# Banded attention moved from a stage of its own into the projection of its layer

## The reference

```
x  = x + 0.5 * norm(swiglu(norm(x)))                  # FFN 1, 2 x 2816 wide
p  = norm(x) @ w_in                                   # 768 + 1032 + 1024 columns
y_attn  = sliding_window_gqa(rope(q), rope(k), v)     # 8 query heads, 2 key heads of 64, window 128, sinks
y_mlstm = mlstm(silu(conv4(q, k)), v, gates)          # 4 heads
y_rwkv  = rwkv7(u + (shift(u) - u) * mu)              # 4 heads; u: the last 1024 columns of p
x  = x + norm(concat(y_attn, y_mlstm, y_rwkv) @ w_out)
x  = x + 0.5 * norm(swiglu(norm(x)));  then a gated embedding term
```

## Time and profile before

| | |
|---|---|
| Median of 3 runs | 3319.95 us (3317.6 to 3321.46) |
| The profiled execution, its own time | 3315.65 us |
| Its span, first to last instruction | 3313.8 us |
| PE busy | 3106.2 us, 94% |
| DVE, ACT, POOL busy | 42%, 33%, 5% |
| Mean granted TensorE clock | 0.950 of full |

### The profile page before, as it was taken

How to read it: one execution, slowest core, us unless ns; L and a number is a source line. 1 busy time by engine, 2 the same in 40 slices (tenths; PEclk the granted TensorE clock), 3 DMA queues, 4 the chain that set the end, 5 groups by cost and what they waited for, 6 DMA issues and landing times. The chain is left out here.

```text
span 3313.8 us, 42013 instructions
## 1 busy us (share of the span) xinstructions
PE 3106.2 (94%) x17718; PEld 2614.0 (79%) x17718; DVE 1385.5 (42%) x1867; ACT 1109.9 (33%) x1566; POOL 175.5 (5%) x145
## 2 busy tenths in 40 slices
PE   8999998877999999999999678899999989999999
PEld 7888886657888888888887548788887878888887
DVE  3333414556333245333332554523326247545542
ACT  3232322333322235232222332422225345434431
POOL 0000004500000000000000630000000000000000
PEclk9999999669999999999999759899999989999999
DMA  3333321001123342233413000223333210112222
GB/s 132 99 96 108 108 64 54 1 9 64 53 89 96 112 130 77 82 96 108 136 36 93 1 9 3 98 69 101 109 103 120 68 46 23 60 61 96 96 96 83
DMA packets 71483, 255.28 MB, mean 77 GB/s; under 512 B 8056, under 2 KB 9208, under 8 KB 71296
## 3 DMA queue, kind: packets, MB, share of 16 engines
q1 hardware_dynamic: 71296, 252.59, 23.8%
HBM read 250.46 MB, written 2.10 MB: 76 GB/s over the span
## 5 line engine op out<-in xcount | busy, mean ns | idle before, releaser
L206 PE MATMUL ps<-h_hi,w_space 128*128 128x512 f32 (+3 forms) x5440 | 1505.2, 363 | 17.1 <-DVE h_lo L304 17.1
L206 PEld LDWEIGHTS ps<-h_hi,w_space 128*128 128x128 f32 x5440 | 981.7, 190 | 177.8 <-DVE h_lo L304 20.3
L194 DVE TENSOR_TENSOR w_space<-w_raw,w_space 128x1024 fp32r<-128x1024 f32 x440 | 536.3, 1225 | 1222.0 <-ACT w_space L187 1221.5
L206 PE MATMUL ps<-h_lo,w_space 128*128 128x512 f32 (+3 forms) x2720 | 986.0, 363 | 0.0
L187 ACT CAST w_space<-w_raw 128x1024 fp32r<-128x1024 f32 x440 | 458.0, 1047 | 1122.1 <-PE ps L206 726.0
L216 PE MATMUL ps<-w_space 128*128 128x512 f32 x3312 | 767.9, 393 | 15.9 <-DVE w_space L194 15.0
L216 PEld LDWEIGHTS ps<-w_space 128*128 128x128 f32 x3312 | 626.5, 190 | 147.6 <-issue 11.6
L206 PEld LDWEIGHTS ps<-h_lo,w_space 128*128 128x128 f32 x2720 | 516.4, 190 | 77.9
L579 ACT CAST w_space<-act_p 128x512 fp32r<-128x512 f32 x88 | 54.6, 621 | 187.4 <-DVE act_p L591 172.4
L594 DVE TENSOR_TENSOR w_space<-act_p,w_space 128x512 fp32r<-128x512 f32 x88 | 61.0, 693 | 69.8 <-ACT w_space L579 69.8
L591 DVE TENSOR_TENSOR act_p<-act_s,ps 128x512 f32<-128x512 f32 x88 | 60.0, 681 | 71.3 <-PE ps L206 71.3
(11 more groups left out here) (324 smaller groups left out, 2732.1 us busy)
## 6 DMA issues: line engine op xcount, KB each, us to landing
w_raw<-in_w_ffn_in SPq DMA_DIRECT2D x176, 512.0 KB, 3.6
w_raw<-in_w_ffn_out SPq DMA_DIRECT2D x88, 512.0 KB, 3.6
w_raw<-in_w_in SPq DMA_DIRECT2D x64, 512.0 KB, 3.7
w_raw<-in_w_up SPq DMA_DIRECT2D x44, 512.0 KB, 3.3
w_raw<-in_w_out SPq DMA_DIRECT2D x24, 512.0 KB, 3.7
w_raw<-in_w_down SPq DMA_DIRECT2D x22, 512.0 KB, 3.3
w_raw<-in_w_ple_gate SPq DMA_DIRECT2D x16, 512.0 KB, 4.8
gain_pre<-in_gains_pre SPq DMA_DIRECT2D x10, 512.0 KB, 4.5
```

The costliest lines, as they stand in the source:

```text
L194: nc.vector.tensor_tensor(self.lo(n), self.raw[:, n % SLOTS, :], self.hi(n).bitcast(F32), ALU.subtract).then_inc(self.lo_ready, 1)
L206: m = nc.tensor.matmul(c.ps[:, bank, t], part[:, cols], moving[:, k, t], start=(k == 0 and i == 0), stop=(k == KD - 1 and i == 2))
```

## The change

The stage is gone. A class `WindowAttention` holds the same operations, with their waits, and a class `MixProj` calls them in numbered steps from the projection: `steps_after(n)` gives the steps that follow tile n. Steps 3 to 5 (constants, rope of k and the first q) follow tiles 3 to 5, one a tile. From tile 6 on there are two steps a tile: the first stands behind tile n and the second halfway through tile n+1, between its matmuls 12 and 13. Step 6+2h is `rough_scores(h)` and `values(h-1)`, step 7+2h is `scores(h)` (and `turn_back` in steps 11, 15 and 19), so the eight heads take the halves of tiles 7 to 14, and values(7) follows tile 14. Tiles 15 to 22 carry no step. The last `turn_back` follows tile 22.

The tiles stand in another order (k, q, v, mLSTM qk, rwkv, mLSTM v, o, gates). From tile 4 on they use two PSUM banks in turn, and attention has the other six; `scores` has one pair of banks, not two. The bodies of `rough_scores`, `values`, `exponents`, `maxima` and `normalise` issue the same instructions as before. The masks are loaded by SP, in the first FFN's down product, into rows of `c.y`. POOL's convolution and its token shift both follow in the projection, tile by tile as these are stored; the token shift leaves the mLSTM stage. ACT now copies a tile out before it splits the next weight unit; before it was the other way round.

```diff
     for k in range(KD):
+        if halfway is not None and k == KD // 2:
+            halfway()
...
+class MixProj(Proj):
...
+    def bank(self, n):
+        return n if n < SLOTS else n % 2
+    def before_in_bank(self, n):
+        return n - 2 if n >= SLOTS + 2 else n - 4
+    def steps_after(self, n):
+        if n < 6:
+            return [n]
+        return [i for i in (2 * n - 6, 2 * n - 5) if i <= 22]
+    def tensor_with(self, pe, nc, attention):
+        for n in range(SLOTS, self.tiles):
+            later = self.steps_after(n - 1)[1:] if n > SLOTS else []
+            self.tensor_tile(pe, nc, n, (lambda: attention.tensor_after(pe, nc, later[0])) if later else None)
+            for i in self.steps_after(n)[:1]:
+                attention.tensor_after(pe, nc, i)
+        attention.tensor_end(pe, nc)
+    def scalar_with(self, act, nc, attention):
         c, W = self.c, self.c.W
-        W.lo_to(dve, nc, self.end())
-        if self.gates:
-            dve.wait_ge(W.done, self.end())
-            for g in range(2):
-                nc.vector.tensor_copy(c.gates[0:4, g, :], c.ps[32 * g:32 * g + 4, self.bank(self.plain), :]).then_inc(c.gates_set, 1)
+        W.hi_to(act, nc, self.u0 + EARLY)
+        for n in range(self.tiles):
+            act.wait_ge(W.done, self.u0 + n + 1)
+            if n < self.plain:
+                nc.scalar.copy(c.proj[:, n, :], c.ps[:, self.bank(n), :]).then_inc(c.stored, 1)
+            if n >= SLOTS:
+                W.hi_to(act, nc, min(self.u0 + n + 3, self.end()))
+            for i in self.steps_after(n):
+                attention.scalar_after(act, nc, i)
+        attention.scalar_end(act, nc)
+    def vector_with(self, dve, nc, attention):
+        c, W = self.c, self.c.W
+        W.lo_to(dve, nc, self.u0 + EARLY)
+        for n in range(SLOTS, self.tiles):
+            W.lo_to(dve, nc, min(self.u0 + n + 3, self.end()))
+            for i in self.steps_after(n):
+                attention.vector_after(dve, nc, i)
+        dve.wait_ge(W.done, self.end())
+        for g in range(2):
+            nc.vector.tensor_copy(c.gates[0:4, g, :], c.ps[32 * g:32 * g + 4, self.bank(self.plain), :]).then_inc(c.gates_set, 1)
...
-R_T, K_T, V_T, WA_T, G_T, AQ_T, AK_T, AV_T, MQ_T, MV_T, MO_T = 0, 2, 4, 6, 7, 8, 12, 13, 14, 18, 20
+AK_T, AQ_T, AV_T, MQ_T, MV_T, MO_T = 0, 1, 5, 6, 18, 20
+R_T = 10
+R_AT, K_AT, V_AT, WA_AT, G_AT = 0, 2, 4, 6, 7
+SPARE = (0, 2, 4, 6, 8, 18, 20)
...
-def window_attention_stage(nc, c, l, window_masks):
...
+class WindowAttention:
...
+    FIRST_BANK, SCORE_BANK, VALUE_BANK, TURN_BANK = 2, 4, 6, 7
+    PARTNER_BANK = (4, 5, 6, 7, 7)
...
+        self.masks = c.y[:, 4:7, :]
...
+    def load(self, sp, ffn):
+        sp.wait_ge(self.c.act_ready, ffn.f0 + KF)
+        sp.wait_ge(self.c.sines, 3)
+        sp.dma_start(self.masks, self.window_masks).then_inc(self.loaded, 16)
...
+    def gpsimd(self, pool, nc):
+        c = self.c
+        pool.wait_ge(c.consts_loaded, 48)
+        self.wait_tile(pool, AV_T)
+        nc.gpsimd.memset(self.v_tok[:, :, :, DH:DH + 1], 1.0).then_inc(self.ones_set, 1)
+        pool.wait_ge(self.consts, 3)
+        conv = Chain(pool, self.conv_chain)
+        tap = lambda n, t: self.vec[:, VEC["conv"] + 4 * n + t:VEC["conv"] + 4 * n + t + 1]
+        for t in range(4):
+            u, out = c.proj[:, MQ_T + t, :], c.y[:, M_QK + t, :]
+            self.wait_tile(pool, MQ_T + t)
...
+        for t in range(KD):
+            u_t, d = c.proj[:, R_T + t, :], (self.tapped, self.shifted)[t % 2]
+            self.wait_tile(pool, R_T + t)
...
+    def scores(self, pe, nc, h):
+        c = self.c
+        if h:
+            pe.wait_ge(self.exps, 2 * h)
+        for b in range(2):
+            bank = self.SCORE_BANK + b
...
+    def tensor_after(self, pe, nc, n):
+        c = self.c
+        if n == 4:
+            pe.wait_ge(c.consts_loaded, 48)
+            self.partner(pe, nc, 0)
+            self.partner(pe, nc, 1)
+        if n == 5:
+            self.partner(pe, nc, 2)
+        if n == 6:
+            self.wait_tile(pe, AV_T)
+            for i in range(NT):
+                m = nc.tensor.transpose(c.ps[:, self.TURN_BANK, i * P:(i + 1) * P], c.proj[:, AV_T, i * P:(i + 1) * P],
+                                        c.mat["ident"])
+            m.then_inc(self.v_turned, 1)
+        if n >= 6 and n % 2 == 0:
+            h = (n - 6) // 2
+            if h < HEADS:
+                self.rough_scores(pe, nc, h)
+            if h == 1:
+                pe.wait_ge(self.v_copied, 1)
+                pe.wait_ge(self.ones_set, 1)
+                pe.wait_ge(self.roped, 3)
+            if h:
+                self.values(pe, nc, h - 1)
+        if n >= 7 and n % 2:
+            h = (n - 7) // 2
+            if h == 0:
+                pe.wait_ge(self.roped, 2)
+            if h == 0:
+                pe.wait_ge(self.v_copied, 1)
+                self.partner(pe, nc, 3)
+            if h == 1:
+                pe.wait_ge(self.roped, 4)
+                self.partner(pe, nc, 4)
+            self.scores(pe, nc, h)
+            if h >= 2 and h % 2 == 0:
+                if h == 2:
+                    pe.wait_ge(self.roped, 5)
+                self.turn_back(pe, nc, h // 2 - 1)
+    def tensor_end(self, pe, nc):
+        self.turn_back(pe, nc, HEADS // 2 - 1)
...
+    def scalar_after(self, act, nc, n):
+        c = self.c
...
+        if n >= 7 and n % 2:
+            h = (n - 7) // 2
+            if h + 2 < HEADS:
+                self.first_of_q(act, nc, h + 2)
+            self.exponents(act, nc, h)
+        if n >= 12 and n % 4 == 0:
+            self.copy_out(act, nc, n // 4 - 3)
...
+    def vector_after(self, dve, nc, n):
+        if n == 4:
...
+        if n >= 6 and n % 2 == 0:
+            h = (n - 6) // 2
+            if h < HEADS:
+                self.maxima(dve, nc, h)
+            if h:
+                self.normalise(dve, nc, h - 1)
+        if n >= 7 and n % 2:
+            h = (n - 7) // 2
+            if h < 2:
+                self.rotate(dve, nc, h + 3)
+            if h == 0:
+                self.rest_of_k(dve, nc, 1)
+            if h + 2 < HEADS:
...
-                for t in range(KD):
-                    u_t, d = c.proj[:, R_T + t, :], shifted[:, t % 2, :]
-                    if t >= 2:
-                        pool.wait_ge(mixed, t - 1)
...
+        attention = WindowAttention(st, c, proj, 0, window_masks)
...
                 c.W.load_to(sp, ffn.down.d0 + SLOTS)
                 proj.turn.load(sp)
+                attention.load(sp, ffn)
                 c.W.load_to(sp, following)
...
-                proj.tensor_rest(pe, nc)
+                proj.tensor_with(pe, nc, attention)
...
-            window_attention_stage(nc, c, l, a["window_masks"])
...
-    pick = np.r_[rwkv_at:rwkv_at + 1024, 0:attn_cols + 1024]
+    pick = np.r_[512:640, 0:512, 640:768, attn_cols:attn_cols + 512, rwkv_at:rwkv_at + 1024, attn_cols + 512:attn_cols + 1024]
```

More of the change, by code:

```diff
@@ new lines, in scores @@
+    def scores(self, pe, nc, h):
+        c = self.c
+        if h:
+            pe.wait_ge(self.exps, 2 * h)
+        for b in range(2):
+            bank = self.SCORE_BANK + b
+            nc.tensor.matmul(c.ps[:, bank, 0:S - b * P], self.ident_r[:, :], self.masks_r[:, 2, 0:S - b * P], start=True,
+                             stop=False)
+            for j in (2 * b, 2 * b + 1):
+                last = min(j + 2, NT)
+                o = c.ps[:, bank, (j % 2) * 2 * P:(j % 2) * 2 * P + (last - j) * P]
+                for k in (self.k_hi, self.k_lo):
+                    nc.tensor.matmul(o, k[:, h // GROUP, j * P:(j + 1) * P], self.q_both[:, h % 3, j * P:last * P],
+                                     start=False, stop=False)
+                if j == 0:
+                    pe.wait_ge(self.diag_ready, h + 1)
+                m = nc.tensor.matmul(o, self.ones_r[:, :], self.diag[:, h % 2, j:last, :], start=False, stop=(j % 2 == 1))
+            m.then_inc(self.scored, 1)
@@ new lines, in values @@
+    def values(self, pe, nc, h):
+        c, g = self.c, h // GROUP
+        pe.wait_ge(self.exps, 2 * (h + 1))
+        if h:
+            pe.wait_ge(self.normed, h)
+        for n in range(NT):
+            o = c.ps[:, self.VALUE_BANK, n * (DH + 1):(n + 1) * (DH + 1)]
+            if n:
+                nc.tensor.matmul(o, self.probs[:, h % 2, n - 1, WIN:2 * WIN], self.v_tok[:, n - 1, g, :], start=True, stop=False)
+            m = nc.tensor.matmul(o, self.probs[:, h % 2, n, 0:WIN], self.v_tok[:, n, g, :], start=(n == 0), stop=True)
+        m.then_inc(self.pv_done, 1)
@@ new lines, in tensor_end, with first_of_q, first_of_k @@
+    def tensor_end(self, pe, nc):
+        self.turn_back(pe, nc, HEADS // 2 - 1)
+    def first_of_q(self, act, nc, h):
+        act.wait_ge(self.roped, h // 2 + 2)
+        if h >= 3:
+            act.wait_ge(self.scored, 2 * (h - 2))
+        half = self.half_of(h)
```

(20 more changed lines are left out.)

481 lines of the change are left out of this document (205 added, 276 removed).

## The result

The changed kernel takes 3259.74 us (median of 4 runs, 3257.23 to 3264.33) against 3320.7 us of the kernel before beside it (4 runs, 3317.6 to 3325.9): a ratio of 0.982, 95% interval 0.9806 to 0.9835. The forecast was 3258.6 us. The profiled execution took 3260.64 us for a span of 3258.8, 55.0 us less than the span before. The median fell by 61.0 us: the profile of the kernel before is of an execution that was 5 us faster than the median of its runs, and that of the changed kernel is not. Two of the six executions of run 9 were in a slower state, the profiled one (4120.65 us) and one of 10913.65 us, and are left out.

A forecast was written before the change was run, and what follows sets the result against it. Attention was taken as a chain of PE, DVE and ACT waiting in turn, the projection as bound by PE alone. -149.1 + 80.8 + 5 + 6 + 1 - 5 = -61.3 us: 3254.3 profiled, median 3258.6, range 3241 to 3284.

The forecast's parts named there:

- The stages removed: Attention stages of both layers, with their barrier, disappear: 74.5 + 74.6 us, -149.1 us.
- PE's added work: Attention's PE work moved into the projection, added in full: 40.4 us a layer, +80.8 us for both.
- The joints: PE's 64 changes between tile and attention in the projection cost some 0.08 us each: +5 us, bounds 0 and 13.
- POOL's lock: POOL delays DVE's `lo` and `neg_top` beside the heads: 3 us a layer, +6 us, bounds 0 and 26.
- the slack: At each head in the projection, PE's cover of 5.61 us against the `diag` chain's 5.07: 0.3 us to spare.
- the rival of the falling clock: Granted clock falls in tiles that carry heads: at half clock in all, 155 us more, 3414 us; chance 0.04.
- SP's masks: Masks in SP's queue delay first-layer FFN weights by some 4 us: +1 us, bounds 0 and 3.
- mLSTM: POOL's token shift leaves the mLSTM stage: 2.5 us a layer gained, -5 us, bounds 0 and 8.
- the rival in which this stage speeds up: Clock holds for the mLSTM stage's first part: 10 to 17 us a layer gained, 3230 us; chance 0.06.
- The late start: DVE and ACT chain in steps 4 to 6 is late at heads 0 and 1: 3268 us; chance 0.08.
- the unhidden attention: An overlooked wait stands ahead of half a tile, only half of PE's idle time goes: 3290 us; chance 0.06.

The follow-up runs named there:

- run 9: Changed kernel with the `stored` base raised by 22 instead of 23 and masks three units later in SP's queue, timed: median 3258.0 us, ratio 0.9799.
- run 4: Changed kernel with POOL's convolution held until tile 14 and the token shift back in the mLSTM stage: 3267.05 us in one run.
- Run 5: Changed kernel with the `stored` base corrected to 22 tiles and one attention step a tile instead of two: 3253.94 us, ratio 0.9797.
- run 3: Changed kernel with both attention steps behind the tile, none halfway in it: 3318.67 us in one run.
- Run 1: Changed kernel with the base of semaphore `stored` raised by its 22 copied tiles instead of 23: 3251.16 us, ratio 0.9783.
- run 6: Changed kernel with the `stored` base corrected and SP loading three more weight units before the masks: 3256.62 us in one run.
- 10: Changed kernel with only the `stored` base corrected to 22 tiles, timed again: 3254.5 us, ratio 0.9788.
- 7: Changed kernel again without an edit, for a second profile: 3257.38 us in one run.
- 8: Kernel before again without an edit, for a third profile: 3323.85 us in one run.

## Why the prediction was right, and where it was not

**The stages removed**, -149.1: measured -149.2 between the first two profiles. In the other two profiles of before this stretch lasted 1.9 and 2.5 us longer, so the row that the term was read from was a short one.

**The total** is in part luck. For the profiled execution the forecast was 3254.3 us and it took 3260.64, mostly by the rwkv stages below. The median was to lie 4.3 above that execution and lay 0.9 below it. These two misses cancel, and 3258.6 came within 1.1 us of 3259.74.

**PE's added work**, 80.8: right. The first layer grows by 41.7 us against 40.4 of counted work. What is left, 1.3 us, holds the joints, POOL's disturbance and every wait.

**The joints**, +5: over-estimated. POOL's part of the 1.3 us is 0.6 (run 4), so at most 0.7 are left for 32 joints, 0.02 each, not 0.08. The row on which I built was one of the old stage, where PE changed from `values` to rough scores, and its 0.32 us were already inside the 1.01 of rough scores, so that this joint was counted twice. In PE's timeline of the changed kernel the first matmul of rough scores behind tile 13 takes 0.23 (526.27 to 526.50), and the first of the tile behind a step 0.31 (528.68 to 528.99): only the way back into the tile costs 0.08. Run 5 has as many joints in more tiles, and the same sum.

**POOL's lock**, +6: measured 1.3 for both layers. The mechanism is there (run 4), and the slack was right too: 0.3 computed, 0.4 by run 3. What was wrong is the average of 0.8 us for the wait. `neg_top` loses 0.37 at most heads, and `lo` keeps its time at six heads of eight, so that a head of the first layer loses 0.4 us on the mean, about the slack. By the Trainium skill (SBUF — State Buffer, Who interferes with whom) DVE and GpSimd instructions that need the shared port pair exclude each other, and the one that starts second waits for the whole of the other. The trace agrees that they disturb each other, but the longest `lo` at these heads lost 0.41 us in the first layer and 0.73 in the second, where most of POOL's instructions last 1.0 to 1.9. So my mean was too near to that rule.

**The missed term**, +8.4: I wrote, against the rival of the falling clock, "Bank n-2 was copied out 5 us before it is wanted, though, so I see no idle time for it here." That is true of the first layer and false of the second, where the wait names n-1. I had read the new `before_in_bank`, but not what the base `s0` counts. Run 1 shows it. Joints and lock together were some 8.4 us too dear, and this made up for it: the agreement of 91.9 with 91.8 is two errors of opposite sign.

**SP's masks**, +1: the late unit came as estimated (294.14), and it cost some 1.5 us of the first layer by the profiles (run 6). In the profile of the changed kernel a higher clock behind it took that back, and the times of runs 9 and 10 can't tell it.

**mLSTM**, -5: measured -6.4, by the mechanism named (run 4). The term was 0.7 us a layer too small: the two scans next to `u` lose time beside POOL too, 1.1 us of the 2.1 read above, and I had priced `u` and L1306 and taken "not all on the chain". The clock of the first mLSTM stage stayed at 0.50 from 588 us on, so the rival in which this stage speeds up did not occur.

**The rwkv stages**, not in the sum: +9.5 in the one profile, and chance as far as runs 1, 7 and 8 tell. Three profiles of before gave 122.94 to 126.90, a mean of 124.5; eight of changed kernels gave 121.90 to 129.82, a mean of 125.7. Whether 1.2 us a stage are real is open.

**The rivals.** The clock did not fall in the head tiles (1.00 in every window of the first layer's, where PE had next to no idle time); in run 3, with waits of 2.3 to 2.7 us at the heads, it did. That rival was real, and what kept it away here is the half tile of cover, with only 0.4 us to spare at each head. I had not connected it with the slack. The Trainium skill (TensorE: Matmul & The Clock Gate, A second HAM failure mode: psum-queue depth-cycling) tells of small idle times from cycling through PSUM banks that make the clock go up and down. In the second layer's tiles 16 to 22 such idle times did occur, but there the trace does not agree. Over 40 us with a gap at every tile the clock stayed at 1.00:

```profile
1789.00:1829.00 40.00, 35.32 (x149) 27.06 (x147) 7.35 (x6) 9.24 (x13) 20.29 (x16) 1.00 0.25 79
```

The late start and the unhidden attention did not occur: no wait of PE for `diag` in the first layer but the 0.3 us, and one of 0.6 in the second.

## What to carry to other kernels

Work that has to run on the engine that bounds the kernel can still be moved under a dense stage if the gaps it had of its own are then filled: here 149 us of stage became 83 us of PE work. The slack of the tightest wait is worth computing to a tenth and then testing by taking its cover away. When a ring of buffers gets shorter, recount every semaphore that guards it, in the second pass through the loop as well as in the first; an off-by-one that eight banks hid cost 1.05 us at each of seven tiles with two. And when a sum comes out right, compare its terms: two layers of one program that differ by 8 us are a better hint than a total that agrees.

## What the runs showed of the hardware that was not expected

- A wait can cost more than itself: with waits of 2.3 to 2.7 us at six heads the granted clock went from 1.00 to a mean of 0.85 over 80 us, some 10.5 us beside the 19.3 of all waits (run 3). PE was busy for 66.02 of these 80 us. With a gap of 0.8 us in every 6.49 us, PE busy for 35.32 of 40, the clock stayed at 1.00.
- A stage whose instructions are the same took 124.02 and 129.82 us in two executions of the same kernel, with the clock falling at different places. One profile is not enough to put some microseconds of such a stage down to a change.
- Beside POOL, DVE's reduction from PSUM kept its 1.22 us and `diag` its 0.69, while `neg_top`, on four values a partition, went from 0.23 to 0.60 at most heads of the first layer. `lo`, 1.23 us, took 1.46 and 1.64 at two of its eight heads, and 1.43 and 1.96 at two of the second layer's.
